# A two-layer diffusion backbone with routed experts: the last expert block copied later, the last squares summed by TensorE, two context chunks modulated by ScalarE

## The reference, cut to what matters

```python
def run_layer(x, mod, attn_fn, lp):
    shift1, scale1, gate1, shift2, scale2, gate2 = jnp.split(mod, 6, axis=-1)
    h = modulate(rmsnorm(x, lp['norm1_g']), shift1, scale1)
    mix, kv = token_mixers(h, attn_fn, lp)          # one 1024 x 8192 projection, four mixers, merge
    x = x + gate1[:, None, :] * mix
    h2 = modulate(rmsnorm(x, lp['norm2_g']), shift2, scale2)
    x = x + gate2[:, None, :] * expert_choice_ffn(h2, lp['w_router'], lp['w1'], lp['w3'], lp['w2'])
    return x, kv

def modulate(h, shift, scale):
    return h * (1 + scale[:, None, :]) + shift[:, None, :]

def rmsnorm(x, g):
    xf = x.astype(jnp.float32)
    y = xf * lax.rsqrt(jnp.mean(xf * xf, axis=-1, keepdims=True) + EPS)
    return (y * g.astype(jnp.float32)).astype(x.dtype)
```

## Time and profile before

| | |
|---|---|
| median of 3 runs | 2993.83 us (2991.87 to 3005.42) |
| the profiled execution's own time | 2993.84 us |
| its span | 2992.0 us |
| mean granted TensorE clock | 0.972 of full speed |
| busy: TensorE, VectorE, ScalarE, GpSimd | 93%, 39%, 23%, 13% of the span |
| chain of waits: TensorE, transfers, VectorE | 66%, 24%, 6% |
| read from memory | 577 MB, 203 GB/s over the span; near 400 GB/s while the experts run |

### The profile page before, as it was taken

How to read it: one execution, slowest core, us unless ns; L and a number is a source line. 1 busy time by engine, 2 the same in 40 slices (tenths; PEclk the granted TensorE clock), 3 DMA queues, 4 the chain that set the end, 5 groups by cost and what they waited for, 6 DMA issues and landing times.

```text
span 2992.0 us, 70745 instructions
## 1 busy us (share of the span) xinstructions
PE 2784.9 (93%) x32716; PEld 2047.5 (68%) x32716; DVE 1179.4 (39%) x1655; ACT 689.3 (23%) x900; POOL 378.9 (13%) x356
## 2 busy tenths in 40 slices
PE   7999999999996999899889999999999869999996
PEld 3555576655753898888745556766566459988895
DVE  3973223332115443333469532233311344433335
ACT  2012023331003232322220120333310113232331
POOL 1330000000001121111125110000000011111111
PEclk9999999999997999999999999999999979999998
DMA  8222301012037999999932221012021359999994
GB/s 356 89 120 113 128 29 62 34 72 108 28 141 286 395 403 396 406 406 405 360 134 113 101 87 60 34 62 87 29 92 74 123 212 385 408 399 400 407 413 174
DMA packets 55634, 608.08 MB, mean 203 GB/s; under 512 B 6464, under 2 KB 6592, under 8 KB 21216
## 3 DMA queue, kind: packets, MB, share of 16 engines
q1 hardware_dynamic: 41504, 555.76, 45.9%
q0 software_dynamic: 7168, 23.47, 3.2%
q10 hardware_dynamic: 6848, 27.27, 2.3%
HBM read 577.25 MB, written 29.23 MB: 203 GB/s over the span
## 4 chain that ended last, share of the span: by engine, by line
PE 66%; DMA 24%; DVE 6%; ACT 2%; issue 2%; POOL 0%; DVEq 0%; ACTq 0%; POOLq 0%
PE ps L417 56%; DMA region_b<-in_w_exp 22%; DVE ring L1530 2%; ACT ring L1230 1%; DMA region_b<-in_w_last 1%; PE ps L702 1%; PE ps L685 1%; PE ps L759 1%; PE ps L740 1%; DVE rstd L1261 1%; PE ps L673 1%; DMA region_b<-h_rows,rstd 1%; PE ps L492 0%; PE ps L606 0%; PE ps L925 0%
## 5 line engine op out<-in xcount | busy, mean ns | idle before, releaser
L417 PE MATMUL ps<-hT,ring 128*128 128x320 f32 (+2 forms) x3480 | 986.4, 441 | 9.3 <-ACT hT L979 9.3
L417 PE MATMUL ps<-region_r,ring 128*64 128x80 f32 x24192 | 902.9, 236 | 68.0 <-ACT ring L1230 41.4
L417 PEld LDWEIGHTS ps<-region_r,ring 128*64 128x64 f32 x24192 | 880.0, 139 | 90.9 <-issue 52.9
L417 PEld LDWEIGHTS ps<-hT,ring 128*128 128x128 f32 x3480 | 591.0, 191 | 358.0 <-issue 225.9
L417 PE MATMUL ps<-region_b,ring 128*128 128x320 f32 (+2 forms) x896 | 257.4, 439 | 2.7 <-issue 2.7
L1329 DVE SCALAR_TENSOR_TENSOR region_b<-region_b,params 128x655 f32<-128x655 f32 x240 | 245.6, 1023 | 8.5
L1530 DVE COPY ring<-region_b 128x4096 f32<-128x4096 f32 x66 | 152.6, 2312 | 222.0 <-DMA region_b<-in_w_exp 109.2
L417 PEld LDWEIGHTS ps<-region_b,ring 128*128 128x128 f32 x896 | 159.3, 191 | 74.7 <-issue 26.9
L1230 ACT ACTIVATE ring<-region_b 128x4096 f32<-128x4096 f32 x28 | 101.3, 3620 | 265.6 <-DMA region_b<-in_w_exp 248.9
L1460 DVE TENSOR_TENSOR sig<-ps,sig 128x640 f32<-128x640 f32 x32 | 26.4, 825 | 323.1 <-PE ps L759 323.1
L417 PE MATMUL ps<-region_x,ring 128*128 128x512 f32 (+1 forms) x480 | 139.4, 449 | 3.8 <-DVE region_x L1464 3.8
(11 more groups left out here) (232 smaller groups left out, 2465.4 us busy)
## 6 DMA issues: line engine op xcount, KB each, us to landing
region_b<-in_w_exp SPq DMA_DIRECT2D x90, 2048.0 KB, 18.5
ring<-in_w_mix SPq DMA_DIRECT2D x61, 2048.0 KB, 9.4
hT<-in_w_exp SPq DMA_DIRECT2D x46, 2048.0 KB, 18.6
region_x<-in_w_exp SPq DMA_DIRECT2D x44, 2048.0 KB
ring<-in_w_ada SPq DMA_DIRECT2D x6, 2048.0 KB, 10.0
ring<-in_w_first SPq DMA_DIRECT2D x6, 2048.0 KB, 8.6
x_store<-region_m ACTq DMA_DIRECT2D x2, 2560.0 KB, 11.0
ffn_rows<-region_r ACTq DMA_DIRECT2D x4, 1280.0 KB, 17.6
```

What stands on the lines that cost most here:

```text
L417: ins = pe.matmul(*args, **kw)
```

## The change

Four edits, with one of them in the order of two engines:

1. VectorE copies block 95 into the ring behind the gate product of half 31, instead of ahead of `copy_y(29)`.
2. TensorE runs block 95 right behind block 94 (with y of half 30 turned between them); the "A" steps come behind block 95, and y of half 31 is turned behind the second step. `copy_y(31)` on VectorE comes ahead of all steps.
3. At a layer's end the square of chunk 7 is no longer added on VectorE: TensorE sums it by four more products in the same PSUM group. The next layer's modulation table is made within step 7.
4. In all four modulated norms ScalarE modulates the context columns of chunks 0 and 1, ahead of the latent ones; GpSimd does chunks 2 to 7.

```diff
+ACT_CHUNKS = 2
...
-    _add += 3 if _key[0] == "conv" or _key[0] == "in" and _key[1] else KC - 1
+    _add += 3 if _key[0] == "conv" else 2 if _key[0] == "in" and _key[1] else KC - 1
...
-                pe.wait_ge(S["square_used"], ADD_AT[key] + 3)
+                pe.wait_ge(S["square_used"], ADD_AT[key] + 2)
                 for b, t0, t1 in columns("half"):
-                    last = pe.matmul(PS[1][:, b, 0:t1 - t0], ones, half_sum[:, t0:t1], start=False, stop=True)
+                    pe.matmul(PS[1][:, b, 0:t1 - t0], ones, half_sum[:, t0:t1], start=False, stop=False)
+                pe.wait_ge(S["squared"], SQ_AT[key] + KC)
+                for b, t0, t1 in columns("half"):
+                    last = pe.matmul(PS[1][:, b, 0:t1 - t0], ones, sq2[:, 1, t0:t1], start=False, stop=True)
...
                 pe.wait_ge(S["h_ready"], KC * NORM_AT[where, l] + k + 1)
-                pe.wait_ge(S["hc_ready"], KC * NORM_AT[where, l] + k + 1)
+                if k >= ACT_CHUNKS:
+                    pe.wait_ge(S["hc_ready"], (KC - ACT_CHUNKS) * NORM_AT[where, l] + k - ACT_CHUNKS + 1)
...
                 for b in range(LAST_BLOCKS):
-                    if b:
-                        for step in range(4):
-                            tail(step)
                     turn_y(HALVES - 3 + b)
                     need("act_ready", HALVES)
                     expert_block(FIRST_BLOCKS + LOOP_BLOCKS + b, 0, y_ps, act, "y_done")
-                turn_y(HALVES - 1)
-                for step in range(4, len(TAIL)):
+
+                for step in range(len(TAIL)):
+                    if step == 2:
+                        turn_y(HALVES - 1)
                     tail(step)
...
+                    if k < ACT_CHUNKS:
+                        sc.activation(h[:, k, LAT:TOK], h[:, k, LAT:TOK], ACT.Identity, scale=msc[:, norm, k, 1:2],
+                                      bias=mod3[:, 24 * norm + k, 1:2])
...
-                    to_ring(w3)
+                    if i < HALVES - 1:
+                        to_ring(w3)
...
                         v.tensor_copy(flat(act)[:, 0:HC], sil[0]).then_inc(S["act_ready"], 2)
+                    if i == HALVES - 1:
+
+                        to_ring(w3)
                 copy_y(HALVES - 2)
+                copy_y(HALVES - 1)
...
-                    if step == 3:
-                        copy_y(HALVES - 1)
+                    if step == 7 and l + 1 < LAYERS:
+                        v.wait_ge(S["params_in"], 16 * (l + 2))
+                        modulation(l + 1, 0, "g1", mod_next)
                     if k >= 6:
+
                         add_later_square(k - 1)
-                if l + 1 < LAYERS:
-                    v.wait_ge(S["params_in"], 16 * (l + 2))
-                    modulation(l + 1, 0, "g1", mod_next)
-                add_later_square(KC - 1)
...
                 for k in chunks:
+                    if k < ACT_CHUNKS:
+                        continue
                     g.wait_ge(S["mod_ready"], mods(l, norm, k))
```

## The result

The changed kernel takes 2977.71 us (median of 5 runs, 2976.7 to 2982.42), the kernel before, on the same chip, 2993.83 (5 runs, 2991.87 to 3005.42): ratio 0.9948, 95% interval [0.9932, 0.9963]. Its profiled execution has a span of 2975.9 us against 2992.0, so 16.1 us less. Forecast were 2981.8 (11.95 us less), with a range of 2976 to 2988.

The account below looks back on a forecast made before the run. TensorE was taken to bound the kernel (two thirds of the span; transfers a quarter), so only its waits for other engines counted. Terms summed to 11.95 us off 2993.84, forecast 2981.8 us, range 2976 to 2988.

Parts of the forecast that it names:

- Copy of block 95: Layer ends: with VectorE's long copy behind the products, block 94 starts 3.69 us (layer 0) and 3.43 us (layer 1) earlier.
- Slack of the long copy: Layer ends: block 95's copy ends at 1470.6 and is wanted at 1474.4; slack is 2.3 us at least.
- Clock: Block 94: with the hole shrunk it keeps full speed and takes 4.57 us, saving 1.04 and 1.65 us.
- The tail's order: Layer ends: gap between blocks 94 and 95 shrinks by 2.78 us, first "AB" step costs 3.36; net 0.58 lost per layer.
- Squares and modulation: Layer ends: TensorE's square sum and the table in step 7, hidden behind a VectorE wait, lose 0.1 us for both.
- Context chunks: Four norms: two chunks on ScalarE gain 1.18 us ahead of layer 1's mixers, 1.3 at the start, 0.92 in routers.
- The first norm: Very start: ScalarE begins with GpSimd, so TensorE starts at 26.2 instead of 27.50, 1.3 us earlier.
- rival C: All goes a little better (1.40 us stop gone, routers, block gap, earlier clock rise): 2978.8 us and below; chance 0.22.
- The routers: Two router stages: GpSimd's shorter train ends them 0.46 us earlier each, 0.92 in all.
- three VectorE products beside one GpSimd instruction: Norms: GpSimd's 2.3 us instruction spans three VectorE products; were it one, router stages would give about 1 us each.
- rival A: Blocks 94 and 95: late instructions cause one to three more TensorE stops, 2983.5 to 2986.5 us; chance 0.18.

Follow-up runs that it names:

- fill_94: Kernel before, plus four unused TensorE products in the hole ahead of block 94: 2991.79 us, ratio 0.9997.
- order_only: Kernel before, with only the tail's "A" steps moved behind block 95, the last y turn behind the second: 2995.31 us, ratio 0.9997.
- squares_only: Kernel before, with only the last square summed by TensorE and the modulation table made in step 7: 2995.93 us, ratio 1.0007.
- act_two: Kernel before, with only the context columns of chunks 0 and 1 moved to ScalarE in all four norms: 2992.2 us, ratio 0.9990.

## Why the prediction was right, and where not

The mechanism of the tails, most of the sum, came as forecast. That the time lies only 4 us off has its luck too: 4.7 us of gains stood in no term (1.4 by a stop that did not come, 3.3 ahead of the tails) and 1.0 was lost by the table; had the two gains been 1.7 us larger, the range would have been missed.

*Copy of block 95.* Right. Forecast 3.69 and 3.43 us; block 94 starts 5.38 - 1.81 = 3.57 and 5.12 - 1.82 = 3.30 us sooner, 0.12 and 0.13 less. Slack of the long copy: it ends at 1465.54, block 95 starts at 1469.19.

*Clock.* Right: 4.57 in both layers, 1.04 and 1.65 us saved, and the filled hole shows the cause.

*The tail's order.* The lengths are right: block 95's end to the first "AB" step is 9.64 us and 9.63, forecast 9.65, at a cost of 3.35 where 3.36 stood; the gap between blocks 94 and 95 is 1.23 us, forecast 1.53. So 0.3 less is lost in each layer. What is wrong is the step's sentence that "the reordering itself brings nothing": true of edit 2 alone, false of its part in the change. Without it the "A" steps would wait 3.2 and 3.6 us for transfers. The sum came out right since the edits were costed together as they stand; the reader of that sentence would have left edit 2 out and lost the whole gain.

*Squares and modulation.* This step failed: "The modulation (0.45) goes into step 7, and behind it VectorE waits 1.45 us for an "AB" step anyway". The table takes 2.95 us there, beside GpSimd's additions, and costs 1.0. The squares' half came out at 0.24 us gained.

*Context chunks.* The first norm gave 1.15 us for 1.3 and 0.99 more by an earlier rise of the clock (the lead is 2.14 us by 35 us), which stood in rival C. The routers gave 0.61 and 0.46, forecast 0.46 each (9.44 and 9.60 us against 10.05 and 10.06), which fits three VectorE products beside one GpSimd instruction and not one. Ahead of layer 1's mixers TensorE starts 2.27 us behind VectorE's first chunk, not 3.34: 1.07 for 1.18; its tile of 11.59 instead of 10.91 us took 0.68 of it back, at the low clock, so this term was 0.4 net in this pair of profiles. That loss is not shown to be the change's: the second execution of the changed kernel takes 10.52.

*What was in no term.* The stop of 1.40 us in layer 0 is gone, as rival C had it. A stop of 1.12 to 2.18 us without releaser stands in layer 0 in both executions of before, fill_94, order_only, squares_only and act_two, beginning at 1482.7 to 1486.1 us whichever code runs there, and in none of the seven executions that have edits 1 and 2 together (in three of these one product of block 95 starts 0.3 to 0.5 us late). The traces show what ends such a stop. The list of transfers has a queue of kind "instruction", and in the kernel before one piece of 16 KB on it starts between 1484.9 and 1485.0; the first row is from a view of 1484.8 to 1485.0, the second is the stop:

```profile
q8 instruction: 1, 0.02, 30.8%
...
1487.44 0.70 PE L417 MATMUL ps<-region_r,ring 128*64 128x80 f32 x14 [1.40 <-issue]
```

It lands at 1485.91, and TensorE goes on 1.54 us later. In the six executions with the stop it goes on 1.47 to 1.61 us behind such a landing. Over the 14 traces all 118 stops without releaser (0.18 to 3.14 us) in the first unrolled expert blocks and in the tails end 1.2 to 1.6 us behind one, while the pieces land mostly 5 to 10 us apart. That points to TensorE waiting there for its own instructions, and so gives rival A's stops a cause; it is read from these times alone, no run moved such a transfer on purpose. Why the piece comes late in some executions and in time in others is not settled.

The 3.3 us of lead at block 93 of layer 0 that were not forecast go with gains of 2.94 and 1.68 us by a clock that fell, or didn't, in gaps that the change doesn't touch, of which the expert blocks took a part back. So the outcome is the forecast's mechanism with a part of rival C's additions (the stop gone, an earlier clock in the first norm, 0.3 less between the blocks), less 1.0 for the table.

## What to carry to other kernels

When a hole between two blocks is closed, look for who is late next in the blocks behind it, transfers included: an edit can be worth nothing alone, its partner nothing alone, and the two 10 us. A hole of 5 us in TensorE's work was paid twice here, by its length and by the granted clock behind it, and cheap unused products in it recovered the second payment. A stop that no engine explains can be held against the transfers of kind "instruction". Before a small instruction is called hidden, ask what the neighbour engines do at that moment. And profile each kernel twice before explaining a difference of 3 us in 3000.

## What the hardware did that was not expected

A VectorE instruction of 0.2 us took 1.40, and one of 0.17 took 1.55, beside GpSimd additions of 1.54 us: each ended within 0.07 us of the end of the GpSimd instruction then running. The additions into x beside the same train, which have one input in PSUM and one in SBUF, kept their 1.14 us a pair.

Behind the same idle gap of 3.14 us the granted clock stayed at full speed in some executions (window mean 1.00) and fell to 1.2 GHz for a part of the next products in others (0.83, 0.67). And in one tail of 28 TensorE went at a mean clock of 0.54 through 14.8 us in which it was busy throughout (10.88 us for products that take 6.47 elsewhere), behind no longer gap than its neighbours had.

Within unrolled code under a full stream of weights TensorE stopped for 0.18 to 3.14 us at a time, and each of 118 such stops ended 1.2 to 1.6 us behind the landing of 16 KB of instructions.
